# The RG-LRU coefficients from an exponential and a product instead of a reciprocal

## The reference

```python
    r = sigmoid(einsum(xh, w_a) + b_a)
    i = sigmoid(einsum(xh, w_x) + b_x)
    log_a = -LRU_C * r * softplus(-lam)
    a = exp(log_a)
    mult = sqrt(maximum(-expm1(2.0 * log_a), 0.0))
    b = mult * i * xc
    h = scan over time of h = a * h + b
```

## Time and profile before

| | |
|---|---|
| median of the runs | 1458.19 us |
| span of the profiled execution | 1455.0 us |
| its own time | not given beside the span |
| PE busy | 1251.6 us (86%) |
| DVE busy | 890.4 us (61%) |
| ACT busy | 516.9 us (36%) |
| POOL busy | 419.3 us (29%) |
| chain that ended last | PE 69%, DVE 16%, DMA 4%, issue 4%, ACT 4% |

### The profile page before, as it was taken

How to read it: one execution, slowest core, us unless ns; L and a number is a source line. 1 busy time by engine, 2 the same in 40 slices (tenths; PEclk the granted TensorE clock), 3 DMA queues, 4 the chain that set the end, 5 groups by cost and what they waited for, 6 DMA issues and landing times.

```text
span 1455.0 us, 23155 instructions
## 1 busy us (share of the span) xinstructions
PE 1251.6 (86%) x6575; PEld 975.4 (67%) x6576; DVE 890.4 (61%) x1751; ACT 516.9 (36%) x907; POOL 419.3 (29%) x438
## 2 busy tenths in 40 slices
PE   6798899999998955999997169999999999985664
PEld 1113899999997944888885048888888888872221
DVE  2013868998988676556555845456664654224886
ACT  1100455544455331222221134445544534222331
POOL 1030122221122245565653311111111111106882
PEclk9898899999999977999997569999999999996896
DMA  8970101110111253343443266757867683316883
GB/s 276 387 272 4 37 1 58 58 58 3 54 58 58 93 190 126 132 153 139 159 133 113 79 231 221 263 210 257 278 229 238 241 277 115 115 77 235 293 291 113
DMA packets 112334, 230.17 MB, mean 158 GB/s; under 512 B 11381, under 2 KB 61049, under 8 KB 112277
## 3 DMA queue, kind: packets, MB, share of 16 engines
q1 hardware_dynamic: 93711, 162.15, 33.3%
q0 software_dynamic: 11680, 42.47, 8.5%
q10 hardware_dynamic: 6912, 25.17, 4.3%
HBM read 169.62 MB, written 60.27 MB: 158 GB/s over the span
## 4 chain that ended last, share of the span: by engine, by line
PE 69%; DVE 16%; DMA 4%; issue 4%; ACT 4%; SPq 2%; POOL 1%; POOLq 0%; DVEq 0%; ACTq 0%
PE bank L1489 18%; PE bank L1491 17%; PE bank L1490 17%; PE bank L1436 6%; PE bank L1463 4%; DVE arena L1400 2%; PE bank L1554 2%; DVE st L1165 1%; DVE arena L1159 1%; PE bank L1510 1%; DVE arena L1409 1%; PE bank L1624 1%; DMA arena<-in_w_in 1%; DVE parts L1092 1%; PE bank L1740 1%
## 5 line engine op out<-in xcount | busy, mean ns | idle before, releaser
L1489 PE MATMUL bank<-parts 128*128 128x256 f32 (+2 forms) x1616 | 569.1, 352 | 25.3 <-POOL parts L571 17.6
L1491 PE MATMUL bank<-parts 128*128 128x256 f32 (+2 forms) x1616 | 552.6, 342 | 0.0
L1490 PE MATMUL bank<-parts 128*128 128x256 f32 (+2 forms) x1616 | 552.0, 342 | 0.0
L1489 PEld LDWEIGHTS bank<-parts 128*128 128x128 f32 x1616 | 308.6, 191 | 63.4 <-POOL parts L571 18.0
L1491 PEld LDWEIGHTS bank<-parts 128*128 128x128 f32 x1616 | 308.1, 191 | 35.8
L1490 PEld LDWEIGHTS bank<-parts 128*128 128x128 f32 x1616 | 309.0, 191 | 31.9
L1436 PE MATMUL bank<-ident,arena 128*128 128x128 f32 (+4 forms) x788 | 118.0, 282 | 26.3 <-DMA arena<-u_d,tok_now 10.4
L1436 PEld LDWEIGHTS bank<-ident,arena 128*128 128x128 f32 (+4 forms) x788 | 94.7, 146 | 53.5 <-issue 15.8
L1740 PE MATMUL bank<-arena 128*128 128x512 f32 (+1 forms) x136 | 80.3, 748 | 50.9 <-ACT arena L925 39.6
L1331 DVE TENSOR_TENSOR parts<-arena,parts x90 | 104.9, 1221 | 17.9 <-ACT parts L859 14.2
L620 POOL COPY tok_now<-tok_i 128x1 int32 (+1 forms) x48 | 9.4, 195 | 364.7 <-PE bank L1436 347.9
(11 more groups left out here) (226 smaller groups left out, 1640.4 us busy)
## 6 DMA issues: line engine op xcount, KB each, us to landing
ada_arena<-in_w_ada SPq DMA_DIRECT2D x12, 2048.0 KB, 11.4
ys_d<-arena ACTq DMA_DIRECT2D x48, 512.0 KB
arena<-in_w_gate SPq DMA_DIRECT2D x16, 1024.0 KB, 6.1
arena<-in_w_up SPq DMA_DIRECT2D x16, 1024.0 KB, 9.8
arena<-in_w_down SPq DMA_DIRECT2D x16, 1024.0 KB, 14.1
arena<-in_x_prompt SPq DMA_DIRECT2D x8, 1024.0 KB, 6.7
yT_d<-arena SPq DMA_DIRECT2D x16, 512.0 KB, 4.4
arena<-yT_d SPq DMA_DIRECT2D x16, 512.0 KB, 4.8
```

The source lines that it names most:

```text
L1489: pe.matmul(out, x_hi, w_hi, start=start, stop=False)
L1490: pe.matmul(out, x_hi, w_lo, start=False, stop=False)
L1491: return pe.matmul(out, x_lo, w_hi, start=False, stop=stop)
```

## The change

Each gate group on ACT gets one Exp more, E = exp(log_a), between the first pair of Tanh and the second Tanh, with a wait for its result, since the second Tanh overwrites the same input. The Sqrt now goes in place, and E has the place of the old root. The per-channel constant of the Exp, sp4n, is made once at the start. On DVE, q = (E + 1) * sqrt(T), b = 0.5 * q * (gated input), and a = 1 - q * sqrt(T), without a reciprocal.

```diff
+        sp4n = sb("sp4n", [P, NG])
...
                     act.wait_ge(S["gates_evac"], 2 * NG * i + 2 * j + 2)
-
+                    act.activation(tE[:, j, 0:n], tT[:, j, 0:n], ACT.Exp, bias=sp4n[:, j:j + 1],
+                                   scale=sp4n[:, j:j + 1]).then_inc(S["E_ready"], 1)
+                    act.wait_ge(S["E_ready"], NG * i + j + 1)
                     act.activation(tT[:, j, 0:n], tT[:, j, 0:n], ACT.Tanh, bias=sp2[:, j:j + 1],
                                    scale=sp2[:, j:j + 1]).then_inc(S["T_ready"], 1)
...
-                    act.activation(tS[:, j, 0:n], tT[:, j, 0:n], ACT.Sqrt).then_inc(S["S_ready"], 1)
+                    act.activation(tT[:, j, 0:n], tT[:, j, 0:n], ACT.Sqrt).then_inc(S["S_ready"], 1)
...
+            o.did(dve.tensor_scalar(sp4n[:], sp_t[:, 4, :], LRU_C / -2, None, ALU.mult))
+            o.wait()
...
                 dve.wait_ge(S["S_ready"], NG * i + j + 1)
-                o.step(dve.tensor_scalar(q_t[:, 0:n], tT[:, j, 0:n], 1.0, None, ALU.add))
-                o.step(dve.reciprocal(q_t[:, 0:n], q_t[:, 0:n]))
+                o.step(dve.scalar_tensor_tensor(q_t[:, 0:n], tE[:, j, 0:n], 1.0, tT[:, j, 0:n], ALU.add, ALU.mult))
                 dve.wait_ge(S["gated_x"], NG * i + j + 1)
-                o.did(dve.tensor_scalar(a_out, q_t[:, 0:n], 2.0, -1.0, ALU.mult, ALU.add))
-                o.step(dve.tensor_tensor(q_t[:, 0:n], q_t[:, 0:n], tS[:, j, 0:n], ALU.mult))
-                o.step(dve.tensor_tensor(b_out, tI[:, j, 0:n], q_t[:, 0:n], ALU.mult))
+                o.did(dve.scalar_tensor_tensor(b_out, q_t[:, 0:n], 0.5, tI[:, j, 0:n], ALU.mult, ALU.mult))
+                o.step(dve.tensor_tensor(a_out, q_t[:, 0:n], tT[:, j, 0:n], ALU.mult))
+                o.step(dve.tensor_scalar(a_out, a_out, -1.0, 1.0, ALU.mult, ALU.add))
```

More of the change, by code:

```diff
@@ L145, in build @@
         gel = at(12936, NG, C)
-        tT, tI, tS = at(13960, NG, C), at(14984, NG, C), at(16008, NG, C)
+        tT, tI, tE = at(13960, NG, C), at(14984, NG, C), at(16008, NG, C)
         q_t, a_t, b_t, h_t = at(17032, C), at(17288, C), at(17544, C), at(17800, C)
@@ L250, in build @@
             wout_lo_pool wout_lo_dve yT_hi_ok yT_lo_ok gate_in proj_ready proj_evac xc_ready xr_free p_free gates_mm
-            gates_evac T_ready T_guard S_ready gated_x h_ready d_ready pool_mm pool_evac ylru_ready y_stored
+            gates_evac E_ready T_ready T_guard S_ready gated_x h_ready d_ready pool_mm pool_evac ylru_ready y_stored
             prj_copied out_mm out_evac out_stored out_s_stored w_out_in tiles_in tiles_s_in rt_in yTt0 yTt1 xres0
@@ L1750, in _ @@
             combine(NT - 1, 0, 0, NT // 4 + 1, NS)
-CHUNK_STEPS = 58
+CHUNK_STEPS = 54
 LN_STEPS = 14
```

## The result

The changed kernel takes 1470.83 us (median of four runs, 1469.37 to 1471.79) against 1457.79 us of the kernel before (four runs, 1456.68 to 1458.48): the ratio is 1.0093, with a 95% interval of 1.0079 to 1.0107. It is 13.0 us slower, where 8.4 were forecast; the time lies in the forecast range. The span of the profiled execution is 1468.5 us, 13.5 more than before.

A forecast was written before the change was run, and what follows sets the result against it. The prediction took ACT's gates, which PE's order 10 waits for, and DVE's recurrence in the bridge as bounds; 14.0 + 0.4 - 0.3 - 5.7 = +8.4 us gave about 1466.6 us, range 1458.5 to 1474.

The forecast's parts named there:

- ACT on the path, +2.00 us a chunk: Chunk gates: four added Exps with waits make ACT's Gelu, and PE's order 10 behind it, 2.00 us later.
- 7 x 2.00 = +14.0: Chunks 1 to 7: each pays the 2.00 us ACT delay in full, +14.0 us together.
- the clock only as a rival: PE's waits before order 10: PE's clock falls in each stall, 2.4 us each, 19 us more, 1486 us; chance 6%.
- Chunk 0, +0.4: Chunk 0: a possible table load and four small Exps on ACT, mostly covered by DVE's pooling sums, +0.4 us.
- Tables: Chunk gates on ACT: no added table cost if Tanh and Exp have one table.
- Chunk 8, -0.3: Chunk 8: ACT's delay is covered by its 2.27 us idle before L726, and weights come earlier, -0.3 us.
- DVE, 1.65 us a group, nothing in the chunks: DVE recurrence: each group 1.65 us shorter, costed at nothing in chunks 1 to 7 because PE waits for ACT.
- Bridge, -5.7: Last four recurrence groups behind chunk 8: shorter DVE groups, less contention with POOL, gain 5.7 us.
- 2.44 + 0.36 = 2.80: Bridge, DVE time per group: 2.44 us for the new instructions plus 0.36 for contention with POOL.
- DVE as the pace: Chunk loop: DVE sets the pace, so the kernel gets 11 us faster, 1447 us; chance 6%.
- the cheap Exp: Chunk gates: the stall is only 1.3 us and the bridge gains 6.8, so no change, 1460.6 us; chance 8%.
- separate tables: Chunk gates: Exp and Tanh need different tables, 10.3 us of loads a chunk, about 1547 us; chance 3%.

The follow-up runs named there:

- the version with the late Tanh: Changed kernel with the second Tanh of all four groups moved behind the second Gelu and first pooling result, no wait behind the Exp: 1449.58 us, ratio 0.9944.
- the DVE half alone: Kernel before with only the new four DVE instructions, ACT without any Exp, recurrence numbers not the reference's: 1449.5 us, ratio 0.9942.
- the ACT half alone: Kernel before with only the Exps and their waits added on ACT, results unread, DVE keeping the reciprocal: 1477.47 us against 1457.17, ratio 1.0134.

## Why the prediction was right, and what it missed

*ACT on the path, +2.00 us a chunk*: right. The gates grew by 1.95 us, PE's wait from 0.18 to 2.13, and a chunk without a fall of the clock by 1.9; the version with the late Tanh removes the wait with the Exps still there. *7 x 2.00 = +14.0*: mis-sized. The stretch grew by 19.8. Of it 13.5 is the wait (7 x 1.92), and 6.3 the clock (1.5 in each of chunks 2, 4 and 6, and 1.8 in the last stretch, of which some may be the low clock that stands there before the change too). I had the clock only as a rival, at every stall and 2.4 us each, and gave it 6%, because a stage with many pauses of PE showed 0.94. The runs show something between: half of the stalls, 1.5 us each. That, and not the ACT term, is the difference of forecast and result: on the span it is 13.5 - 8.4 = 5.1 us, of which the clock is 6.3 and all the other terms together -1.2. The time lies in the range by luck: no term of the range held the clock, and its upper end came from costs that did not come.

*Chunk 0, +0.4*: right. Up to the first gates of the chunks it is +0.1, but the stages ahead of chunk 0 vary more than that: its first table load on ACT comes at 145.45 us in the kernel before, 145.26 in the changed one and 147.38 with the DVE half alone. From this load to the first gates it is 37.34 us before, 37.63 changed, so +0.3, and 37.73 with the ACT half alone. The Exp there did bring a table load of its own. *Tables*: one for Tanh and Exp, as the Trainium skill ("ScalarE: Activation LUTs", section "Table sets: the hidden batching unit") has it; the trace agrees, with one load per chunk for the sixteen Tanh and Exp of its gates.

*Chunk 8, -0.3*: -0.4; ACT no longer waits before the output weights. *DVE, 1.65 us a group, nothing in the chunks*: right; the DVE half alone leaves the period at 43.6. *Bridge, -5.7*: -5.5. Groups came at 2.85 us, for 2.44 + 0.36 = 2.80. Three of the four new instructions have two inputs, where the prediction counts two; the old five had two. The second instruction takes 0.85 instead of 0.43 us, and ends 0.28 us behind POOL's product (558.08 against 557.80). The Trainium skill ("SBUF — State Buffer", section "Who interferes with whom") has two-input instructions blocked by a GpSimd one that reads SBUF. The trace agrees, but the price is 0.42 us rather than POOL's whole 0.80, which began 0.23 us ahead of it, beside the first instruction.

*Rivals*: DVE as the pace is refuted by the DVE half alone, the cheap Exp by the 0.60 us of L741, and separate tables by the trace.

## What to carry to other kernels

Half-idle says nothing: ACT was 49% busy in a chunk and had no slack in the one place where PE waited for it, and DVE was 90% busy and a fifth of that could go without effect. So the question for an added instruction is which wait ends behind it on its own queue, and the cure is to move it behind that wait: the order of two functions on ACT decided between -7.6 and +13.0 us. And a stall has a second price, since PE's clock may fall behind it; count it where the stall is near the lengths at which the traces show a fall.

## What the runs showed of the hardware

In this loop PE's clock did not fall behind 0.18 or 0.9 us of waiting; it fell behind four of eight waits of 2.13 us in the changed kernel and five of eight with the ACT half alone, and behind all eight of 4.7 us. Which of eight equal waits it falls behind differs between these two kernels (2, 4, 6 and 7 in the one, 3, 4, 6, 7 and 8 in the other, one traced execution each); what picks them was not tried and stays open. Four idle matmuls ahead of the wait, which left 0.40 us of it, were enough to keep the clock at 1.00. And the table that is loaded for the Gelu serves Tanh but not Exp: in chunk 0 of the changed kernel the first Tanh (L738) runs on it without a load and the Exp (L741) loads another, as the timeline of ACT shows, and a chunk's late Tanh needs none.

```profile
145.26 1.28 ACT L772 ACT_TABLE_LOAD   x1
...
147.46 0.54 ACT L738 ACTIVATE arena<-bank,half_b 128x64 f32<-128x64 f32 x2 [0.53 <-PE bank L1514]
148.01 1.28 ACT L741 ACT_TABLE_LOAD   x1
149.31 0.44 ACT L741 ACTIVATE arena<-arena,sp4n 128x64 f32<-128x64 f32 x1
```
